# A decoder step on one core: one wait for all sixteen hidden tiles ahead of the down-projection, in place of one wait per half

## What is computed

```
def sqrelu_ffn(h, w_up, w_down):
    return jnp.square(jax.nn.relu(h @ w_up)) @ w_down
...
xp = xp + sqrelu_ffn(rmsnorm(xp, norm_ffn[layer]), ffn_w_up[layer], ffn_w_down[layer])
```

## Time and profile before

| | |
|---|---|
| median of 3 executions | 1678.48 us (1674.67 to 1684.21) |
| profiled execution, its own time | 1684.21 us |
| its span, first to last instruction | 1682.4 us |
| TensorE busy | 1520.3 us (90%) |
| GpSimd busy | 610.9 us (36%) |
| mean granted TensorE clock | 0.938 |

### The profile page before, as it was taken

The page is one execution under the profiler, slowest core; times in us unless marked ns, Lnnn a source line. Parts: engine busy times, 40 slices in busy tenths (PEclk is TensorE's granted clock), DMA queues, the critical chain, the costliest instruction groups (busy, mean ns, idle before and its releaser), DMA issues.

```text
span 1682.4 us, 28122 instructions
## 1 busy us (share of the span) xinstructions
PE 1520.3 (90%) x12031; PEld 1396.7 (83%) x12031; DVE 698.1 (41%) x993; ACT 472.0 (28%) x882; POOL 610.9 (36%) x276
## 2 busy tenths in 40 slices
PE   6868877688799999999999989998867999999998
PEld 6756654455599999999999989997737999999998
DVE  4757761688435410133112475214565541024212
ACT  4225542233333221122221111103624222122222
POOL 2302203144334653565433442321002664356541
PEclk9969996699899999999999999988868999999999
DMA  4266403487334354354344455436920454444421
GB/s 148 71 219 220 136 26 114 161 303 290 115 121 151 126 199 150 125 199 149 126 150 151 166 192 174 148 139 204 323 99 26 136 189 151 152 173 150 148 78 51
DMA packets 123371, 258.53 MB, mean 154 GB/s; under 512 B 7137, under 2 KB 104561, under 8 KB 116945
## 3 DMA queue, kind: packets, MB, share of 16 engines
q1 hardware_dynamic: 117136, 219.49, 38.2%
q0 software_dynamic: 6144, 37.75, 6.0%
HBM read 249.62 MB, written 95.58 MB: 205 GB/s over the span
## 4 chain that ended last, share of the span: by engine, by line
PE 80%; DVE 10%; ACT 3%; DMA 3%; issue 3%; POOL 1%; SPq 1%; DVEq 0%; ACTq 0%
PE ps L501 21%; PE ps L505 20%; PE ps L502 20%; PE ps L760 4%; PE ps L667 2%; PE ps L704 1%; DVE sq L1587 1%; ACT sc L2085 1%; PE ps L901 1%; PE ps L678 1%; PE ps L779 1%; DMA dv<-q_scratch 1%; PE ps L1004 1%; PE ps L733 1%; DVE KT L1455 1%
## 5 line engine op out<-in xcount | busy, mean ns | idle before, releaser
L2132 POOL TENSOR_TENSOR whl<-wraw,whl 128x2048 fp32r<-128x2048 f32 (+3 forms) x127 | 446.6, 3525 | 580.9 <-ACT whl L1797 580.9
L501 PE MATMUL ps<-hA,whl 128*128 128x260 f32 x1248 | 337.7, 290 | 19.2 <-POOL hA L2132 13.7
L502 PE MATMUL ps<-hA,whl 128*128 128x260 f32 x1248 | 332.9, 287 | 0.0
L1797 ACT ACTIVATE whl<-wraw 128x2048 fp32r<-128x2048 f32 (+3 forms) x127 | 185.9, 1485 | 458.1 <-PE ps L505 396.5
L501 PE MATMUL ps<-uT,whl 128*128 128x260 f32 x1024 | 268.5, 283 | 0.0
L502 PE MATMUL ps<-uT,whl 128*128 128x260 f32 x1024 | 266.3, 281 | 0.0
L501 PEld LDWEIGHTS ps<-hA,whl 128*128 128x128 f32 x1248 | 242.1, 194 | 21.3 <-POOL hA L2132 15.4
L505 PE MATMUL ps<-hA,whl 128*128 128x260 f32 x1248 | 256.6, 288 | 0.0
L502 PEld LDWEIGHTS ps<-hA,whl 128*128 128x128 f32 x1248 | 242.5, 194 | 0.1
L505 PE MATMUL ps<-uT,whl 128*128 128x260 f32 x1024 | 206.8, 283 | 0.0
L505 PEld LDWEIGHTS ps<-hA,whl 128*128 128x128 f32 x1248 | 196.6, 193 | 0.0
(11 more groups left out here) (290 smaller groups left out, 2032.7 us busy)
## 6 DMA issues: line engine op xcount, KB each, us to landing
out_ds<-in_state SPq DMA_DIRECT2D x32, 2047.0 KB, 10.4
wraw<-in_w_up SPq DMA_DIRECT2D x32, 1024.0 KB, 5.6
wraw<-in_w_down SPq DMA_DIRECT2D x32, 1024.0 KB, 5.2
wraw<-in_w_qkv SPq DMA_DIRECT2D x18, 1024.0 KB, 7.3
out_ds<-in_state SPq DMA_DIRECT2D x8, 2044.0 KB, 13.0
dv<-in_state SPq DMA_DIRECT2D x36, 256.0 KB, 6.3
dv<-q_scratch SPq DMA_DIRECT2D x6, 1024.0 KB, 7.1
wraw<-in_w_omla SPq DMA_DIRECT2D x4, 1024.0 KB, 5.1
```

The source lines that it names most:

```text
L501: pe.matmul(ps[:, 2 * u + a, 0:HALF], hi(k), rhs(k, 0)[:, c], start=first, stop=False)
L502: pe.matmul(ps[:, 2 * u + a, 0:HALF], hi(k), rhs(k, 1)[:, c], start=False, stop=False)
L1797: ins = act.activation(dst(0), src, ACT.Copy)
L2132: return pool.tensor_tensor(dst, src, hi.bitcast(F32), ALU.subtract)
```

## The change

TensorE now waits once, ahead of the down-projection, until all sixteen hidden tiles of the half are split. Before, it waited there for the first eight, and for all sixteen ahead of each `kk` 1 chunk; these waits within the loop are gone. Nothing changes on another engine, and no matmul is added, removed or put elsewhere in the order.

```diff
                     loop(pe, vw, 4 if hf else 3, {"w": 2, "tile_summed": 4},
                          lambda i: [linear(KC, 2, MC, h_ffn) for _ in range(2)])
-                    uppers = vw.tick("a", 16)
-                    pe.wait_ge(tile_low, uppers - KC)
+                    split_ready(16)
 
                     def down(i):
                         for m in range(2):
...
                                 if kk == 0:
                                     pe.wait_ge(tile_taken, vw.at("tile_summed", 2))
                                     us = [(vw.n["tile_summed"] + mt) % 4 for mt in range(2)]
-                                else:
-                                    pe.wait_ge(tile_low, uppers)
                                 for mt in range(2):
```

## The result

The changed kernel takes 1707.05 us (median of 4, 1704.61 to 1708.23) against 1680.18 us for the kernel before (median of 4 on the same chip; 1678.48 was the median of the three executions shown ahead of the prediction). The ratio is 1.0158, 95% interval 1.0139 to 1.0177, so it is slower by 26.5 us; 1702 us and a loss of 23.6 us were forecast. The profiled execution of after has a span of 1707.1 us.

What follows compares the result with a forecast made beforehand. TensorE was taken to bound the kernel. Per half, 4.13 us of pause, 1.6 us of low clock and 0.16 us of array filling made 5.9 us; four halves, 23.6 us, on 1678.5 us gave 1702 us, range 1692 to 1710.

Steps and rivals of the forecast that it cites:

- The bound: In the MLP's up- and down-projections TensorE is always busy and alone late, so a pause put there is not absorbed.
- The waits taken out: Sixteen waits ahead of the kk 1 chunks, at most 0.3 us in all if removed; taken as 0.
- The pause: Ahead of each half's down-projection TensorE waits for GpSimd's last tile: 4.13 us a half, 16.5 us in all.
- The clock behind the pause: After each new wait TensorE falls to 1.2 GHz for a stretch, losing 1.6 us a half.
- The first matmul behind the pause: First down-projection matmul after each new wait takes 0.58 us instead of 0.42 as the array fills: 0.16 us more.
- The sum: Four halves at 5.9 us each: 23.6 us more, 1.4%, giving 1702 us.
- the clock holds: Rival: TensorE stays at full clock after each new wait, only latency paid, 4.2 us a half, 1695 us; chance 0.15.
- each pause is followed by a low stretch like the worst of before: Rival: 1.2 GHz lasts as long as at 1004 us, 7.1 us a half, 1707 us; chance 0.09.
- the wait hardly bites: Rival: last tile's path shrinks while TensorE is silent, or lost time is caught up later; about 1680 us, chance 0.04.
- The waits in the loop: Rival: the 16 removed waits each cost more than 1.5 us, so the change is faster, near 1670 us; chance 0.02.
- The length of pause behind which the clock falls: At the four new waits: 4.1 us is twice 2.09 us, the shortest after which it fell, so it falls every time.
- Waits elsewhere: TensorE's waits outside the MLP end on results that follow from TensorE, so they shift with it and recover nothing.

## Why the prediction was right

The direction, the mechanism and the place were right, and 1707.05 us lies in the range of 1692 to 1710. The forecast of 1702 was 5 us short, of which 1.7 us is the kernel before (1680.18 us and not 1678.48) and the rest a loss that was put too low. The terms, in the order of the prediction:

- **The bound.** That TensorE alone sets the time of the MLP, and that nothing absorbs a pause there, held: the local difference between the pauses is 0.0 us.
- **The waits taken out**, costed at 0: shown. Kept beside the new wait, they change neither the time (1.0156 against 1.0158) nor the local cost.
- **The pause**, 4.13 us a half: measured 4.36, 17.4 in all against 16.5. The four operations have their durations of the earlier trace rows, GpSimd's 1.29 for 1.31. What was mis-sized is the hand-over to TensorE, taken as 0.05 us from the earlier trace rows, where no loop follows the wait. With the loop's entry and two further waits behind it, it was 0.32; the wait moved into the loop gave 0.17 of this back.
- **The clock behind the pause**, 1.6 us a half: it fell at all four, as forecast. The slow stretches are 5.1, 5.2, 3.4 and 4.8 us, mean 4.6, where the prediction's loss of 1.6 stood for 3.6. At 0.45 us lost for each this is 8.3 us in all against 6.4. This is the term that was mis-sized most: four of the five stretches it was averaged from, 2.7 to 3.3 us, are shorter than any of the four here. Two of them, at 461 and at 1270, show no fall at all: in the trace of before the clock was at 0.50 ahead of these pauses already (from 453.8 and from 1238.9 us on), so they show only how much of a low stretch was left. The one of 8.74 us was therefore no evidence that a pause makes the clock fall. The four short ones alone would have given 1.3 us; the long one, which has a second pause in it that ours have not, brought the mean nearer, and that part was luck. Filling the pause took 8.0 us off, so that it is the clock is shown; that the same pause brings 3.4 us at one place and 5.2 at another was measured and not explained.
- **The first matmul behind the pause**, 0.16 us: 0.58 us against 0.42 at three places, as in the earlier trace rows. At the third, where the clock had not yet fallen, it is 0.38 against 0.28. That makes 0.6 us in all.
- **The sum**, 23.6 us: with the measured terms 17.4 + 8.3 + 0.6 = 26.3, against a local cost of 26.1 and 26.5 by the times.
- **The rivals.** That the clock holds is what the filled pause shows: 1694.92 us, where 1695 was put. That each pause is followed by a low stretch like the worst of before did not happen (6.2 us there, at most 5.2 here). That this rival's 1707 us is the measured time is chance: it stood for 7.1 us a half, and 6.0 to 6.8 were measured. That the wait hardly bites happens one tile earlier: waiting for fifteen costs 3 us. The waits in the loop are worth nothing.
- **The length of pause behind which the clock falls.** The prediction argued that a pause of twice 2.09 us must make the clock fall. It did, but the ground was weaker than it seemed: at 2.65 us the clock fell at two pauses of four.
- **Waits elsewhere.** Other waits were to shift along with TensorE. Those of layer 1's attention part did not repeat exactly: the longest one for `dk` is 8.5 us in place of the earlier trace rows's 3.08 (followed there by another pause of some 3 us), and the part as a whole is 3.6 us shorter in this one execution of after. In the profiled executions of the seven experiments that leave that part alone it is 2.8 to 6.4 us shorter too, so the one of before was a long one there. It has no bearing on the change.

## What to carry to other kernels

A wait that asks for more than the next instruction needs is free only as long as what it asks for is ready; here the first chunk's 11.5 us of work covered a latency of 4.1, and asking for the last tile ahead of that chunk took the cover away. Price such a pause on a saturated TensorE as its length plus what the work at 1.2 GHz behind it loses, here about 2 us (1.4 to 2.8) for pauses of 4 and of 9 us, and look for a way to keep TensorE at work where a pause can't be avoided. Count the code between a wait and the instruction that it holds back, too: a loop's entry and two waits behind it cost 0.17 us a pause here.

## What the hardware showed that was not expected

- A pause of 2.65 us made the clock fall at two of four places, one of 4.0 us or more at all eighteen in the MLPs, and one of 0.55 us at none. How long TensorE then works at 1.2 GHz does not grow with the pause: 3.4 and 6.1 us behind the two of 2.65, 3.4 to 5.7 behind those of 4.0 to 4.2 in four kernels, 2.8 to 6.0 behind those of 9.0. Nor need it have fallen when TensorE restarts: behind the changed kernel's third pause it fell 0.6 us later.
- The clock fell, and stayed low, while TensorE was busy. The sixteen matmuls of L1004, which have 8 rows and 512 columns, kept TensorE busy for 13.98 of 14.0 us at 0.50 in the kernel before, and in the kernel with the filled pauses the clock fell in their midst, 3.3 us after they had begun at 1.00 behind a pause of 1.2 us. Behind 88 matmuls of 128 rows in a row, which compute nothing of use, it was still 1.00. Whether the shape of the sixteen or the pause ahead of them brought the fall was not tested.
- Matmuls of no use in a pause cost almost nothing by themselves (in the four pauses of the MLPs the next real matmul started under 0.1 us later for them), and 127 of them made the kernel before 0.35% faster.
